# A two-layer streaming encoder on one core: rebuilt stage ends and a moved softmax step

## The reference, cut to what matters

```python
def ada_norm(x, c, w, b, g):
    m = jax.nn.silu(c) @ w + b
    shift, scale, gate = jnp.split(m[:, None, :], 3, axis=-1)
    return rmsnorm(x, g) * (1 + scale) + shift, gate

# per layer l: (l = 0: even_mixer, differential attention (A) and sliding window (B);
#               l = 1: odd_mixer, banded attention with relative bias (C))
hp, gp = ada_norm(xp, c_prompt, ada_w[l, 0], ada_b[l, 0], norm_g[l, 0])
hs, gs = ada_norm(xs, c_sample, ada_w[l, 0], ada_b[l, 0], norm_g[l, 0])
...                      # q, k, v = h @ w_in; p = softmax(q k^T * scale + mask); y = (p v) @ w_out
xp = xp + gp * yp
xs = xs + gs * ys
hp, gp = ada_norm(xp, c_prompt, ada_w[l, 1], ada_b[l, 1], norm_g[l, 1])
...                      # fp, fs = conv_ffn(h): up-projection, causal conv, silu gate, w_down
xp = xp + gp * fp
```

## Time and profile before

| | us |
|---|---|
| median of 3 runs | 3838.22 (3826.9 to 3847.3) |
| the profiled execution | 3831.94 |
| its span, first to last instruction | 3830.4 |
| TensorE busy | 3472.2 (91%), mean granted clock 0.94 |
| VectorE busy | 2121.8 (55%) |
| ScalarE busy | 1347.3 (35%) |
| GpSimd busy | 484.4 (13%) |

### The profile page before, as it was taken

The page is one execution under the profiler, slowest core; times in us unless marked ns, Lnnn a source line. Parts: engine busy times, 40 slices in busy tenths (PEclk is TensorE's granted clock), DMA queues, the critical chain, the costliest instruction groups (busy, mean ns, idle before and its releaser), DMA issues. The chain is left out here.

```text
span 3830.4 us, 54306 instructions
## 1 busy us (share of the span) xinstructions
PE 3472.2 (91%) x20953; PEld 2052.5 (54%) x20953; DVE 2121.8 (55%) x3554; ACT 1347.3 (35%) x2665; POOL 484.4 (13%) x1018
## 2 busy tenths in 40 slices
PE   6878888876889999999989999999798999999998
PEld 3545555544555555555545666556565555555555
DVE  5655555555465555555474555555456555555556
ACT  6644444444232221222234545444433222122221
POOL 1012222232000000000001222222200000000000
PEclk8889888988989999999989989999898999999999
DMA  9723222222311111111121433333521111111111
GB/s 356 264 69 90 63 74 74 66 63 62 100 35 46 43 41 45 39 45 40 39 69 49 123 118 124 121 124 118 175 63 39 46 45 39 39 45 45 40 45 56
DMA packets 222128, 303.87 MB, mean 79 GB/s; under 512 B 24340, under 2 KB 174152, under 8 KB 221315
## 3 DMA queue, kind: packets, MB, share of 16 engines
q1 hardware_dynamic: 191938, 190.39, 15.3%
q0 software_dynamic: 30016, 111.15, 9.6%
HBM read 264.76 MB, written 63.95 MB: 86 GB/s over the span
## 5 line engine op out<-in xcount | busy, mean ns | idle before, releaser
L96 PE MATMUL psum<-h,ffn_high 128*128 128x512 f32 (+1 forms) x2016 | 987.8, 530 | 2.8 <-ACT u L890 2.8
L98 PE MATMUL psum<-hl,ffn_high 128*128 128x512 bf16 (+1 forms) x2016 | 615.5, 339 | 0.0
L100 PE MATMUL psum<-h,ffn_low 128*128 128x512 bf16 (+1 forms) x2016 | 562.2, 333 | 0.0
L96 PE MATMUL psum<-actr,ffn_high 128*128 128x512 f32 (+1 forms) x960 | 470.3, 530 | 7.3 <-DVE xT L604 7.3
L96 PEld LDWEIGHTS psum<-h,ffn_high 128*128 128x128 f32 x2016 | 390.0, 193 | 82.3 <-ACT u L890 3.0
L98 PEld LDWEIGHTS psum<-hl,ffn_high 128*128 128x128 bf16 x2016 | 196.7, 98 | 412.1 <-issue 356.1
L86 PE MATMUL psum<-h,attC_high 128*128 128x384 f32 x744 | 361.4, 486 | 27.3 <-DMA hl<-act_low_dram 9.2
L950 DVE TENSOR_SCALAR y<-u,cvT 128x1168 f32<-128x1168 f32 x88 | 78.1, 888 | 517.7 <-ACT u L895 517.6
L86 PE MATMUL psum<-h,attAB_high 128*128 128x384 f32 x648 | 317.7, 490 | 32.1 <-DMA hl<-act_low_dram 12.9
L98 PE MATMUL psum<-actl,ffn_high 128*128 128x512 bf16 (+1 forms) x960 | 294.1, 340 | 0.0
L182 ACT CAST ffn_high<-ffn_raw 128x1024 fp32r<-128x1024 f32 x130 | 137.2, 1055 | 397.6 <-PE psum L100 388.3
(11 more groups left out here) (514 smaller groups left out, 7299.1 us busy)
## 6 DMA issues: line engine op xcount, KB each, us to landing
ada_raw<-in_ada_w SPq DMA_DIRECT2D x48, 1024.0 KB, 8.7
ffn_raw<-in_w_up SPq DMA_DIRECT2D x88, 512.0 KB, 3.8
ffn_raw<-in_w_down SPq DMA_DIRECT2D x44, 512.0 KB, 3.6
raw_C<-in_cache_c_k POOLq DMA_DIRECT2D x64, 256.0 KB, 3.7
raw_C<-in_cache_c_v POOLq DMA_DIRECT2D x64, 256.0 KB, 3.4
out_ck_s<-in_cache_c_k POOLq DMA_DIRECT2D x8, 1984.0 KB, 8.9
...
```

What stands on the lines that cost most here:

```text
L96: return pe.matmul(out, w, x[:, lo:hi], start=first and start, stop=last and stop, skip_group_check=True)
L98: return pe.matmul(out, top(w), xl[:, lo:hi], start=first and start, stop=last and stop, skip_group_check=True)
L100: return pe.matmul(out, wl, top(x[:, lo:hi]), start=first and start, stop=last and stop, skip_group_check=True)
```

## The change

**1. Raw buffers.** Two raw weight buffers (`G.raws`) are shared by all rings. SyncE loads the first two chunks of the next stage at the end of the attention stages and of ffn 0, once the last chunks of the stage are split; the loads at the next stage's start go. The first attention stage still loads at its own start.

```diff
+def first_up(ins, x):
+
+    l, gate = x // 2, x % 2
+    return ins["w_up"][l].rearrange("(k p) n -> p k n", p=P)[:, :, gate * HALO:gate * HALO + P]
...
                 c, t = chunks(i)
-                up(i, c, t, 0, 0)
+                early = isinstance(i, int) and i == 0
+                if not early:
+                    up(i, c, t, 0, 0)
...
-                up(i, c, t, 0, 1)
+                if not early:
+                    up(i, c, t, 0, 1)
...
+            if l == 0:
+                for x in range(2):
+                    j = (AB_CHUNKS + x) % 2
+                    c = fb + FCH - 3 + j
+                    sp.wait_ge(ring.low[c % 3], c // 3 + 1)
+                    sp.dma_start(rows_by_k(G.raws[j]), first_odd(ins, x)).then_inc(S.t_landed[j], 16)
...
                     if n < KT - 1:
                         mm.then_inc(S.d_ready, 1)
+                    if is_last(i) and n == 6:
+                        pe.wait_ge(S.st_evac, NG * (l + 1))
+                        sums_pe(pe, S, G, "ffn", m + 1, sq, 0)
...
             down(fb + FCH - 2, 0, NG - 1)
-            pe.wait_ge(S.st_evac, NG * (l + 1))
-            for n in (0, 6, 7):
-                sums_pe(pe, S, G, "ffn", m + 1, sq, n, n == 0, n == 7)
+            for g in (1, 2):
+                sums_pe(pe, S, G, "ffn", m + 1, sq, g)
...
             ch.base, ch.n = start + per * (NG - 2), 0
             body(NG - 1)
             down_evac(NG - 1, fb + FCH - 2, 0, 0, KT)
+            squares_dve(dve, S, "ffn", m + 1, sq, KT - 1)
```

```diff
-    scaled_s = ch.mark(dve.tensor_tensor(t4, x4, G.gs[:, m, :, 1:NC9].unsqueeze(3).broadcast_to([P, KT, NB, NS]), ALU.mult))
...
     for lo, hi in ((0, 4), (4, TB)):
         dve.tensor_tensor(d3[:, lo:hi, :], ident.unsqueeze(1).broadcast_to([P, hi - lo, P]),
                           G.rstd9[:, lo:hi].unsqueeze(2).broadcast_to([P, hi - lo, P]), ALU.mult).then_inc(S.diag, 1)
+    scaled_s = ch.mark(dve.tensor_tensor(t4, x4, G.gs[:, m, :, 1:NC9].unsqueeze(3).broadcast_to([P, KT, NB, NS]), ALU.mult))
+    ring.split_low(dve, c)
     dve.wait_ge(S.root, m + 1)
 
...
     scaled(0)
     scaled(1)
-    ring.split_low(dve, c)
     low(0)
     ring.split_low(dve, c + 1)
```

```diff
-SQ_AT = {"att": (0, 1, 2, 3, 1, 2, 4, 1), "ffn": (0, 1, 2, 1, 2, 1, 3, 2)}
-SQ_INTO = {"att": {1: 0, 2: 0, 4: 3, 5: 3}, "ffn": {1: 0, 2: 0, 3: 0, 4: 0, 5: 0}}
+SQ_GROUPS = {"att": ((0, 1), (2, 3), (4, 5), (6, 7)), "ffn": ((0, 1, 2, 3), (4, 5), (6, 7))}
+SQ_AT = {"att": (0, 1, 2, 3, 1, 3, 4, 3), "ffn": (0, 1, 2, 3, 1, 2, 3, 2)}
 SQ_BASE = (None, 0, 4, 9, 13)
 LAG = 4
...
+def group_head(stage, n):
+
+    return next(g[0] for g in SQ_GROUPS[stage] if n in g)
...
 def squares_dve(dve, S, stage, m, sq, n):
 
-    if n in SQ_INTO[stage]:
-        into = sq[SQ_INTO[stage][n]]
+    head = group_head(stage, n) if n >= 0 else n
+    if head != n:
+        into = sq[SQ_AT[stage][head]]
...
         dve.tensor_tensor(into, into, sq[SQ_AT[stage][n]], ALU.add).then_inc(S.sq_added, 1)
```

```diff
+        tail = E[:, 1280:2304] if odd else E[:, 2048:3072]
...
+            for x in range(2):
+                sl, n = ring.at(next(c for c in (cb + total - 2, cb + total - 1) if c % 2 == x))
+                sp.wait_ge(ring.low[sl], n + 1)
+                sp.dma_start(rows_by_k(G.raws[x]), first_up(ins, 2 * odd + x)).then_inc(S.f_landed[x], 16)
...
             pe.wait_ge(S.act_low, un(TL, UNITS - 1))
             for n in range(KT):
-                pe.wait_ge(S.out_evac, 4 * KT * odd + 3 * KT + max(0, n - 1))
-                mm = mm9(pe, ps, 3 * (n % 2), w[:, n * P:(n + 1) * P], wl[:, n * P:(n + 1) * P],
-                         h[:, 7, :], hl[:, 7, :], True, True)
+                mm = mm3(pe, ps[:, 4 + n // 4, n % 4 * P:(n % 4 + 1) * P], w[:, n * P:(n + 1) * P], wl[:, n * P:(n + 1) * P],
+                         h[:, 7, SEQ:TOK], hl[:, 7, SEQ:TOK], n % 4 == 0, n % 4 == 3)
+            mm.then_inc(S.out_ready, 1)
+            for n in range(KT):
+                if n != 1:
+                    pe.wait_ge(S.out_evac, (4 * KT + 1) * odd + 3 * KT + n)
+                for b in range(2):
+                    lo, hi = COLS[b]
+                    mm = mm3(pe, ps[:, 2 * (n % 2) + b, :], w[:, n * P:(n + 1) * P], wl[:, n * P:(n + 1) * P],
+                             h[:, 7, lo:hi], hl[:, 7, lo:hi], True, True)
                 mm.then_inc(*((S.out_ready, 1) if n < KT - 1 else (S.t_used[(cb + total - 1) % 2], 1)))
-                if n == 5:
-                    sums_pe(pe, S, G, "att", m + 1, sq, 0, True, False)
-            for n in (3, 6, 7):
-                sums_pe(pe, S, G, "att", m + 1, sq, n, False, n == 7)
+                if n in (4, 6):
+                    sums_pe(pe, S, G, "att", m + 1, sq, n // 2 - 2)
+            for g in (2, 3):
+                sums_pe(pe, S, G, "att", m + 1, sq, g)
...
 
             run(dve, do)
+            dve.wait_ge(S.out_ready, 3 * KT * odd + 2 * KT + 1)
+            gated = tail.rearrange("p (n b q) -> p n b q", n=KT, b=NB)
+            ch.then(dve.tensor_tensor(gated, ps[:, 4:6, :].rearrange("p x (n b q) -> p (x n) b q", n=4, b=NB),
+                                      G.mod[:, a, 16:24, 1:NC9].unsqueeze(3).broadcast_to([P, KT, NB, NS]), ALU.mult))
+            x = G.xT[:, :, SEQ:TOK]
+            dve.tensor_tensor(x, x, tail.rearrange("p (n t) -> p n t", n=KT), ALU.add).then_inc(S.out_evac, 1)
             for n in range(KT):
                 if n < KT - 1:
-                    dve.wait_ge(S.out_ready, (3 * KT - 1) * odd + 2 * KT + n + 1)
+                    dve.wait_ge(S.out_ready, 3 * KT * odd + 2 * KT + 1 + n + 1)
                 else:
                     ring.done(dve, cb + total - 1)
-                residual(dve, ch, S, G, n, a, 3 * (n % 2), rtmp[:, n % 2, :]).then_inc(S.out_evac, 1)
+                x = G.xT[:, n, 0:SEQ]
+                dve.scalar_tensor_tensor(out=x, in0=ps[:, 2 * (n % 2):2 * (n % 2) + 2, :].rearrange("p b n -> p (b n)"),
+                                         scalar=G.mod[:, a, 16 + n, 0:1], in1=x, op0=ALU.mult,
+                                         op1=ALU.add).then_inc(S.out_evac, 1)
                 squares_dve(dve, S, "att", m + 1, sq, n - 1)
+            squares_dve(dve, S, "att", m + 1, sq, KT - 1)
 
 
```

```diff
-        one, two = ([0], [0]) if last and u < 3 else ([4], [4])
-        body += [("FA", u - 1)] if u else []
+        one, two = ([0], [0]) if last and u < (5 if kind == "B" else 4) else ([4], [4])
...
         body += ([("N", u - 2)] if lag == 2 and u > 1 else []) + turned[0:2]
-        body += ([("O", u - lag)] if u >= lag else []) + two + turned[2:]
+        body += ([("O", u - lag)] if u >= lag else []) + ([("FA", u)] if scored else []) + two + turned[2:]
```

38 lines of the change are left out of this document (24 added, 14 removed).

## The result

The changed kernel takes 3803.2 us in the median of 8 runs (3786.35 to 3812.2), the kernel before 3832.32 in 8 runs beside them (3819.54 to 3847.3): ratio 0.9916, 95% interval 0.9891 to 0.994. Of the 22.5 us between the forecast of 3825.7 and the 3803.2, 5.9 come from the level it started at, the median of three runs (3838.22 against 3832.32 over eight). The profiled execution has a span of 3802.8 us against 3830.4, 27.6 less.

The account below looks back on a forecast made before the run. TensorE, busy 91% of the span at mean granted clock 0.94, was taken as the bound, so only its waits counted. The terms sum to -12.5 us, from the median 3838.22 to 3825.7, range 3808 to 3845.

Parts of the forecast that it names:

- the rest, 0.05: Leftover chance 0.05: another order of stalls in T7 or T15, or the granted clock in C lower by new gaps.
- T5: Tile T5, softmax factors: two rotations now come behind the factors, -1.4 us each, -2.8 in all.
- attention ends: Ends of attention AB and C: one last group of sums left instead of two, -3.7 and -5.1 us.
- ffn ends: Ends of ffn 0 and ffn 1: first sums now ahead of the matmuls of n = 7, +2.7 and +2.1 us.
- My own sign of being wrong: Stage C coming out shorter than about 7 us less than its end and start gain would show the forecast wrong.
- The factors in C: Tiles T8 to T14, pass 7: moved softmax factors start the product with V 1.2 us later, +8.2 in all.
- rival D: Slower than before: factors also bite in passes 5 and 6 of C, +16.8, 3842.5 us, chance 0.12.
- B: Rival: the factors cost nothing in C, the pass being held by something else later; 3817.5 us, chance 0.17.
- E: Rival: moved passes do not fit in the last tiles' stall, so without the 6.4; 3832.1 us, chance 0.08.
- Stage starts: Operations leave the awaited VectorE chain: 2.1 us gained each in ffn 0, attention C, ffn 1, 1.2 in AB; -7.5.
- Rival C: Clock stays at 2.4 GHz in the last sums, four groups at 2.0 instead of 3.84; 3818.3 us, chance 0.13.
- Later output steps: Last tiles T7 and T15: passes moved ahead of the first output step fit in its stall, -3.6 and -2.8 us.

Follow-up runs that it names:

- x6_ffn_sums_back: Changed kernel with the ffn stages' sums of squares as before (squares 1 to 5 added to 0; sums of 0, 6, 7 at the end): 3804.65 us, ratio 0.991.
- x12_later_outputs_only: Kernel before with only the output steps of T7 and T15 later (pass 5 and 4 instead of 3): 3823.46 us, ratio 0.9972.
- x1_fa_back_in_c: Changed kernel with the softmax factors of kind C back at their old place, behind piece 2 of the turned block: 3815.59 us, ratio 0.9954.
- x2_fa_only_in_c: Kernel before with one edit, the softmax factors of kind C moved ahead of piece 2 of the turned block: 3824.51 us, ratio 0.998.
- x7_filled_wait: Kernel before with seven overwritten transposes on TensorE ahead of the wait for the probabilities of each sample block in C: 3804.75 us, ratio 0.9918.

## Why the prediction was wrong, step by step

**The failed step** is the sum's tacit one: it took the granted clock of the tiles of C as given. The forecast read a mean granted clock of 0.94 for the kernel, added up waits as if the move could not change it, and put the clock there under "the rest, 0.05", and only as a loss. Measured: 115 us at the lower level became 47, -24.5 us. Without it the profiled execution would be 3.1 us shorter instead of 27.6. Of the 9.4 from there to my 12.5, 2.9 lie ahead of attention AB's start, in the setup, which the change does not touch, 3.3 in the tiles of AB (below, T5; and 209 us at the lower level instead of 202), 1.6 are the attention ends and 1.3 the ffn ends. My own sign of being wrong came true: stage C is 19 us shorter beyond its end and start. The view was there: two tiles of equal instructions, 96.35 and 104.90 us, with 1.00 and 0.90. I read the mean of 0.94 and did not ask where it came from.

**The factors in C**: +8.2, right in place and size: the wait is 1.25, the tile 1.2 longer at equal clock, passes 5 and 6 pay nothing (neither rival D nor B came; E did not either, see the output steps). The sign of the whole effect was wrong: -16 in the seven tiles with the clock.

**Stage starts**: -2.1 each; -2.3, -2.1, -1.9, and -1.1 for AB (from VectorE's first operation to the product 11.08 before, 9.98 after; -1.2 forecast). The rows that answer to the earlier trace rows, changed kernel:

```profile
1107.24 1.43 DVE L563 TENSOR_TENSOR y<-consts,rstd 128x512 f32<-128x512 f32 x2
1108.59 1.22 DVE L565 TENSOR_TENSOR y<-xT,gs 128x1024 f32<-128x1024 f32 x1
1109.72 1.22 DVE L189 TENSOR_TENSOR ffn_low<-raws,ffn_high 128x1024 bf16<-128x1024 f32 x1
1111.86 2.47 DVE L572 SCALAR_TENSOR_TENSOR u<-xT,gs,psum 128x1024 f32<-128x1024 f32 x2 [0.92 <-PE psum L537]
```

Both operations lie in the wait for the spread root, of which 0.92 is left. ScalarE splits its first chunk at 1106.86 instead of waiting for a DMA.

**Attention ends**: -3.7 and -5.1 forecast, -2.9 and -4.3 measured. The chain stands as laid out, but 0.8 longer. TensorE, answering to the earlier trace rows:

```profile
1079.69 0.30 PE L86 MATMUL psum<-h,attAB_high 128*128 128x128 f32 x1 [1.56 <-DVE hl L2112]
...
1094.88 2.06 PE L513 MATMUL psum<-ones,f_v_AB 128*128 128x1 f32 x18
...
1098.27 2.06 PE L513 MATMUL psum<-ones,f_k_AB 128*128 128x1 f32 x18
1102.39 4.00 PE L513 MATMUL psum<-ones,sw_AB 128*128 128x1 f32 x18 [2.06 <-DVE sw_AB L501]
```

The last sums begin 22.7 behind the start (22.1 forecast) and last 4.0 (3.84). Rival C did not happen: the sums kept TensorE at work until 1100.3, but the wait ahead of the last group stayed (2.06, where it was 1.97); the clock fell in it, and the group ran at the lower level. The rule behind C (the Trainium skill, TensorE: Matmul & The Clock Gate, "Why this matters for your kernels") asks to avoid long idle gaps between bursts of matmuls. It was not put to the test, since the gap was not filled, and it speaks of longer gaps than these: here the clock fell at a wait of 2.06 us, and in C behind waits of 1.04 and 1.12. In this the measurement goes beyond the Trainium skill; the filled wait in C agrees with its direction.

**Ffn ends**: +2.7 and +2.1; 3.6 and 2.7 between the traces of the changed kernel and of `x6_ffn_sums_back`. In ffn 0 the first sums (1962.67, 2.06) stand ahead of n = 7, the last residual starts at 1968.55, and:

```profile
1971.06 1.36 DVE L501 TENSOR_TENSOR y<-y 128x1152 f32<-128x1152 f32 x1 [1.23 <-ACT y L489]
...
1972.47 4.00 PE L513 MATMUL psum<-ones,y 128*128 128x1 f32 x18 [2.59 <-DVE y L501]
```

The mechanism is as forecast: three links in a row, where before TensorE summed square 7 directly. From the residual to the end it is 7.9 instead of 6.9.

**Later output steps**: -3.6 and -2.8. The waits that answer to the earlier trace rows:

```profile
975.09 0.66 PE L86 MATMUL psum<-h,attAB_high 128*128 128x384 f32 x1 [1.22 <-DMA hl<-act_low_dram]
...
2754.43 0.66 PE L86 MATMUL psum<-h,attC_high 128*128 128x384 f32 x1 [11.09 <-DMA hl<-act_low_dram]
```

The step behind is shorter, by a little more than forecast: from the first output step to the final stretch T7 takes 104.6 us instead of 109.7, and T15 131.0 instead of 134.8 (130.3 in `x12_later_outputs_only`). The picture of the waits was half right. In T7, where 9 us of wait should be left, 1.2 is: the two passes, with their own waits and at the lower clock, fill nearly all of the stall. In T15 6 should be left. Where C keeps its long stretches, it is so, 5.2 in `x1_fa_back_in_c` and here in `x12_later_outputs_only`:

```profile
2770.10 0.66 PE L86 MATMUL psum<-h,attC_high 128*128 128x384 f32 x1 [5.21 <-DMA hl<-act_low_dram]
```

In the changed kernel TensorE comes earlier, by the clock, and waits longer, 11.1. The first output step stands 69.1 us behind the start of the tile's sample part, where it stood at 68.6 (68.8 and 69.0 in those two): the DMAs set it. They are issued 40.7 us behind that start instead of 44.5, and land no earlier, 28.3 us after the first issue instead of 24.0.

**T5**: -2.8 was forecast, and next to nothing came. The waits of 1.99 and 1.83 became 0.56 and 0.56, but others came in their place:

```profile
832.94 0.66 PE L1703 MATMUL psum<-consts,E_AB 128*128 128x128 f32 x4 [0.56 <-DVE E_AB L2195]
835.20 0.38 PE L1819 MATMUL psum<-k_AB,q_AB 64*128 64x256 f32 x2 [0.56 <-DVE st_AB L2168]
838.01 0.39 PE L116 MATMUL psum<-W_AB,v_AB 128*128 128x256 f32 x1 [0.94 <-DVE Wl_AB L2074]
839.56 0.66 PE L1703 MATMUL psum<-consts,E_AB 128*128 128x128 f32 x4 [0.56 <-DVE E_AB L2195]
844.18 0.38 PE L116 MATMUL psum<-W_AB,v_AB 128*128 128x256 f32 x1 [1.88 <-DVE Wl_AB L2074]
845.72 1.11 PE L1703 MATMUL psum<-consts,E_AB 128*128 128x128 f32 x4 [0.56 <-DVE E_AB L2195]
```

Before, the product at 840.18, which answers to 844.18, waited 0.61. Between the same two turnings (822.48 to 841.73 before, 826.57 to 845.72 after) lie 19.25 and 19.15 us, both at the upper level nearly throughout. VectorE has as much to do as before, and TensorE waits for it one step further on. The forecast named the waits that go, and did not follow the order to those that come.

**What stays open.** Why one place of the waits keeps the clock up and another does not can't be read from these traces: two tiles with the same instructions and the same waits, 96 us apart, differ. The states of a tile are few and repeat, so it is no noise, but none of the runs says in advance which one an edit will give. One rival is left untested: that what counts is when in time a wait falls, against something that runs on by itself. Then the length of a tile would decide which states follow one another, and a pause, a moved step and an earlier start would all act alike. The first tiles of `x6_ffn_sums_back` and `x2_fa_only_in_c`, slower than those of the changed kernel with the same order in C, would fit that; `x7_filled_wait` shows that TensorE's work in the wait counts whichever it is.
